# A hybrid decoder step on one core: index scores and top-k of the attention layer moved into its projection blocks

## What is computed

```python
q, k, v, qi, ki, wi = jnp.split(rms_norm(x, g) @ w_in, splits, axis=-1)
q, k = rms_norm(q per head, q_norm), rms_norm(k per head, k_norm)
ki, wi = rms_norm(ki, kidx_norm), wi * (N_IDX_HEADS ** -0.5)
# indexer: 8 heads of 64; the prompt in tiles of 128 queries
dots = einsum('bqhd,bld->bqhl', qi, ki) * (IDX_DIM ** -0.5)
s = where(k_pos <= q_pos, einsum('bqh,bqhl->bql', wi, relu(dots)), -inf)
_, idx = lax.top_k(s, topk)      # prompt: 128 of up to 528; sample: 256 of 2049
o = softmax(q . k[idx]) . v[idx]  # 16 query heads, 4 key heads of 64
x = x + o @ w_attn_out
```

## Time and profile before

| what | us |
|---|---|
| three runs | 2703.45, 2711.70, 2712.51 (median 2711.70) |
| the profiled execution, its own time | 2706.93 |
| its span, first to last instruction | 2705.0 |
| PE busy | 2500.7 (92%) |
| DVE busy | 1299.5 (48%) |
| ACT busy | 733.2 (27%) |
| POOL busy | 780.4 (29%) |
| granted TensorE clock, mean of the span | 0.932 |
| DMA | 250.51 MB, mean 93 GB/s |

### The profile page before, as it was taken

One profiled execution on the slowest core, in us unless ns is written; L12 is line 12 of the kernel. 1 busy time (PEld: TensorE's weight loads), 2 busy tenths in 40 slices (PEclk: granted clock), 3 DMA queues, 4 the chain that ended last, 5 costly groups with the idle time before them and its releaser, 6 DMA issues.

```text
span 2705.0 us, 48495 instructions
## 1 busy us (share of the span) xinstructions
PE 2500.7 (92%) x19842; PEld 2357.9 (87%) x19842; DVE 1299.5 (48%) x1810; ACT 733.2 (27%) x1061; POOL 780.4 (29%) x467
## 2 busy tenths in 40 slices
PE   8999999994399999999999999999979729999999
PEld 8999999861166899999999999999978519999999
DVE  5333354337855353333543333677568753433333
ACT  4122132111033232222322222323656322222222
POOL 3311340024200433123533033400653353331130
PEclk9999999956579999999999999999989759999999
DMA  4323232124422122222322322323440002222222
GB/s 151 101 93 109 78 110 94 47 81 131 134 94 94 63 79 85 86 95 75 111 80 80 105 85 73 133 92 124 149 188 31 32 0 93 94 88 82 94 81 91
DMA packets 60998, 250.51 MB, mean 93 GB/s; under 512 B 9376, under 2 KB 25888, under 8 KB 41056
## 3 DMA queue, kind: packets, MB, share of 16 engines
q1 hardware_dynamic: 56672, 223.94, 23.9%
q0 software_dynamic: 4224, 25.17, 2.8%
HBM read 233.58 MB, written 15.49 MB: 92 GB/s over the span
## 4 chain that ended last, share of the span: by engine, by line
PE 85%; POOL 6%; DVE 4%; issue 3%; ACT 2%; DMA 0%; DVEq 0%; POOLq 0%; ACTq 0%
PE acc L592 49%; PE acc L622 22%; POOL kic L723 2%; PE acc L1689 1%; PE acc L773 1%; PE acc L925 1%; POOL xT L2109 1%; PE acc L934 1%; PE acc L815 1%; PE acc L945 1%; PE acc L1736 1%; PE acc L789 1%; PE acc L914 1%; PE acc L1729 1%; POOL wl L2100 1%
## 5 line engine op out<-in xcount | busy, mean ns | idle before, releaser
L592 PE MATMUL acc<-xh,wh 128*128 128x268 f32 (+1 forms) x3616 | 741.1, 286 | 20.3 <-DVE xl L404 16.4
L592 PE MATMUL acc<-xl,wh 128*128 128x268 f32 (+1 forms) x3616 | 740.8, 286 | 0.0
L592 PE MATMUL acc<-xh,wl 128*128 128x268 f32 (+1 forms) x3616 | 738.5, 285 | 0.0
L592 PEld LDWEIGHTS acc<-xh,wh 128*128 128x128 f32 x3616 | 562.9, 189 | 21.8 <-issue 16.3
L592 PEld LDWEIGHTS acc<-xh,wl 128*128 128x128 f32 x3616 | 563.9, 189 | 0.0
L592 PEld LDWEIGHTS acc<-xl,wh 128*128 128x128 f32 x3616 | 563.1, 189 | 0.0
L395 DVE TENSOR_TENSOR wl<-raw,wh 128x2048 fp32r<-128x2048 f32 x185 | 431.2, 2331 | 203.4 <-ACT wh L336 203.4
L336 ACT ACTIVATE wh<-raw 128x2048 fp32r<-128x2048 f32 x194 | 370.5, 1910 | 544.2 <-PE acc L622 411.0
L547 POOL TENSOR_TENSOR gh<-scr,ones 128x536 f32 (+1 forms) x88 | 94.5, 1074 | 950.1 <-DVE scr L424 950.1
L417 DVE TENSOR_TENSOR scr<-acc,rstd 128x536 f32<-128x536 f32 (+1 forms) x88 | 62.7, 713 | 513.9 <-PE acc L592 513.8
L622 PE MATMUL acc<-gh,wh 128*128 128x268 f32 (+1 forms) x1408 | 288.2, 286 | 0.9 <-POOL gl L548 0.9
(11 more groups left out here) (380 smaller groups left out, 2730.5 us busy)
## 6 DMA issues: line engine op xcount, KB each, us to landing
raw<-in_w_ffn_in SPq DMA_DIRECT2D x88, 1024.0 KB, 4.8
raw<-in_w_ffn_out SPq DMA_DIRECT2D x32, 768.0 KB, 4.2
raw<-in_w_ssd_in SPq DMA_DIRECT2D x21, 1024.0 KB, 4.8
raw<-in_w_ffn_out SPq DMA_DIRECT2D x32, 640.0 KB, 3.9
raw<-in_w_attn_in SPq DMA_DIRECT2D x9, 1024.0 KB, 4.8
kic<-in_kpages SPq DMA_DIRECT2D x64, 128.0 KB, 3.0
xT<-in_state_ssm SPq DMA_DIRECT2D x8, 1024.0 KB, 8.2
out_hs<-xT SPq DMA_DIRECT2D x8, 1024.0 KB, 6.0
```

The source lines that it names most:

```text
L592: mm = nc.tensor.matmul(acc[:, slot * 4 + 2 * t + h, 0:(N - lo) // 2], w[:, slot, c:c + P], x[:, kt, half_of(lo, h)], start=(kt == 0 and w ...
```

## The change

The index queries (chunks 6 and 7) and the index key with the head weights (chunk 8) are made first, then the query, key and value chunks (`IN_ORDER`). From the fourth block on PE goes tile by tile, each tile with two PSUM banks of its own (4, 5 or 6, 7) in place of two blocks of four, so banks 0 to 3 are free for index work, written between the 8 steps of a tile. The index key's norm no longer goes with the other heads: it has its own square, sum, root and inverse within block 3, and the sum over 10 tiles is left. Dots of query tiles 1 and 2 stand in the tiles of block 4, cached dots in blocks 5 and 6, dots of tile 3 in block 7, those of tile 4 behind the blocks. The 16 top-k rounds of tiles 1 and 2 and seven of tile 3 stand between DVE's work for the blocks, the other nine of tile 3 behind them. The 32 counting steps are left with the 16 rounds of tile 4, one in each of the first 16 steps. The transposes of values come behind the dots of tile 4, with waits of PE for the copies between them. Loops of the blocks and of SP's sample keys are written out. Semaphores of the second mixer are renamed or joined, without a change in its order.

```diff
+    IN_ORDER = [6, 7, 8, 0, 1, 2, 3, 4, 5]
+        def tile(p, t, beside=None):
+            n = ATT_IN + p
+            if t == 0:
+                pe.wait_ge(wl_ready, n + 1)
+                pe.wait_ge(tile_read, p - 3) if p > 3 else pe.wait_ge(epilogue_done, ATT_IN + 2 + CREDIT)
+            elif p > 3:
+                pe.wait_ge(epilogue_done, n + CREDIT)
+            for kt in range(DT):
+                mm = products(n, kt, t, 4 + 2 * t)
...
+                if beside:
+                    beside(kt)
+        def dots(j, i):
...
+            if v == 16:
+                pe.wait_ge(own_read, 1)
...
+        block(0, 2)
+        pe.wait_ge(std_ready, norm + 1)
+        block(1, 2)
+        block(2, 1)
+        tile(3, 0, index_keys)
+        turn_weights()
+        tile(3, 1)
+        pe.wait_ge(hw_copied, 2)
...
+        tile(4, 0, lambda kt: dots(1, kt))
+        tile(4, 1, lambda kt: dots(2, kt))
+        tile(5, 0, lambda kt: cached_dots(0, kt))
+        tile(5, 1, lambda kt: cached_dots(2, kt))
+        tile(6, 0, lambda kt: cached_dots(4, kt))
+        tile(6, 1, lambda kt: cached_dots(6, kt))
+        own_dots()
+        tile(7, 0, lambda kt: dots(3, kt))
+        tile(7, 1)
+        tile(8, 0)
+        tile(8, 1)
+        pe.wait_ge(sdots_read, 1)
+        for i in range(NIH):
+            dots(4, i)
...
+        pe.wait_ge(v_copied, 1)
...
+        pe.wait_ge(relu_done, 4 * NIH)
         for n, t in enumerate(NORMED):
...
+        rest(6)
+        rounds(1, 0, 11)
+        out(5, 0)
+        rounds(1, 11, 16)
+        rounds(2, 0, 6)
+        out(5, 1)
+        rest(7)
+        rounds(2, 6, 13)
+        out(6, 0)
+        rounds(2, 13, 16)
+        out(6, 1)
+        rest(8)
+        own_product()
+        weighted(3)
+        out(7, 0)
+        cached_products()
+        sample_keys()
+        out(7, 1)
+        rest(9)
+        rounds(3, 0, 3)
+        out(8, 0)
+        rounds(3, 3, 7)
+        out(8, 1)
+        weighted(4)
...
+        rounds(3, 7, 16)
+        dve.wait_ge(headsq, len(NORMED) + 1)
...
-        for j, q0, w in QTILES:
+        for n in range(32):
+            if n < TOPK_P // 8:
...
+                found = largest(4)
```

More of the change, by code:

```diff
@@ L1195, in dve_attention, with rest, out @@
-        for j, q0, w in QTILES:
+        def rest(p):
+            dve_rest(dve, ATT_IN, 0, p)
+        def out(p, t):
+            n = ATT_IN + p
+            if p > 2 and t == 0:
+                dve.wait_ge(tile_done, p - 2)
+            else:
+                dve.wait_ge(chunk_done, n + 1 + CREDIT)
+            bank = (4 if p > 2 else n % 2 * 4) + 2 * t
+            last = t == 1 or p == 2
+            nc.vector.tensor_tensor(halves(hT[:, 2 * IN_ORDER[p] + t]), acc[:, bank:bank + 2, 0:H], halves(rstd[:]), ALU.mult
+                                    ).then_inc(epilogue_done if last else tile_read if p > 2 else dve_side, 1)
@@ new lines, in rounds, with picked, index_keys @@
+        def rounds(j, first, last):
+            for r in range(first, last):
+                chain.after(take_away(j, largest(j)))
+        def picked(j):
+            _, q0, w = QTILES[j - 1]
+            row = bias[:, j - 1, 0:w]
+            chain.link(nc.vector.tensor_scalar(row, score_row(j), GONE / 1.5, -BIG, ALU.is_gt, ALU.mult))
+            if j == 1:
+                nc.vector.tensor_tensor(row[:, q0:w], row[:, q0:w], negm[:], ALU.add).then_inc(dve_side, 1)
+        def index_keys():
+            dve.wait_ge(ki_sq, 2)
+            chain.link(nc.vector.reciprocal(scr[:, 1], scr[:, 1]))
+            nc.vector.scalar_tensor_tensor(halves(kid[:]), acc[:, 0:2, 0:H], headg[:, 2:3], halves(scr[:, 1]), ALU.mult, ALU.mult
+                                           ).then_inc(ki_ready, 1)
@@ L1237, in dve_attention @@
+        for j in range(1, 4):
+            picked(j)
         dve.wait_ge(sdots_read, 1)
@@ L2281, in _ @@
             if what == "attn":
[L2282 to L2286 removed]
                 act.wait_ge(consts_loaded, 64)
+                act_attention_in(act)
                 act_attention(act)
```

575 lines of the change are left out of this document (313 added, 262 removed).

## The result

The changed kernel takes 2740.34 us (median of four runs, 2738.54 to 2742.49), the kernel before 2708.84 us beside it. The ratio is 1.0106, with a 95% interval from 1.0094 to 1.0118: slower by about 1%, or 31.5 us, where 2675 us and a gain were forecast. The profiled execution took 2738.54 us, with a span of 2736.7.

What follows compares the result with a forecast made beforehand. PE was taken to bound the blocks, key gathers the raw scores, DVE the last counts. Raw scores 21.5 us earlier plus 13.5 saved at the end gave 2706.9 - 35 = 2672, stated as 2675; eight-in-ten range 2656 to 2704.

Steps and rivals of the forecast that it cites:

- rival (a): Blocks: clock falls to half from block 4 to the start of block 7, 72 us become 144; 2744, chance 0.06.
- The term "cached dots": Blocks: cached dots moved onto PE's path, 28.4 us at half clock, so 14.2 if the clock stays full.
- The dots of tiles 1 to 3: Blocks: these dots add 12 us to PE's path at full clock, between bounds of 8.7 and 12.0.
- The wait for `rank`: Blocks, tile 3's first dot in block 7: new PE wait for DVE's own product, 3.5 us, at most 5.
- VectorE costs nothing in the blocks: Blocks: DVE's 68 us from the fourth block on delay nothing, each output being 3 to 4 us early.
- Behind the blocks: From the end of the blocks at 545 us to the first raw scores at 608: 63 us forecast.
- the vnew wait: Behind the blocks, at the value turns: PE newly waits for DVE's copy, 2.3 us.
- Raw scores: First to last raw scores: bound by the samples' key gathers, 69.4 us, unchanged.
- rival (c): Counting stage: key loads are no bound and it shortens with the top-k; 2638, chance 0.06.
- Last raw scores to last count: End of counting: eight counts without top-k rounds, 1.3 us a step, 13.5 us saved.
- Rival (b): Behind the blocks: clock already falls there, head sums take 18.4 us; 2680, inside the forecast's 0.74.
- (e): Whole change: it does not do what it says; only a new unseen wait is left, 2700.

Runs made afterwards that it cites:

- e5_wide: Changed kernel with each cached dot given 64 columns instead of 8, same number and places; 0.9982 of the kernel before.
- e1_no_cached: Changed kernel without the 128 cached dots, eight matmuls of 128 columns standing in; 0.9895 of the kernel before.
- e4_neither: Changed kernel without the 128 cached dots and without the 39 top-k rounds in the blocks; 0.9848 of the kernel before.
- e13_repeat_late: Changed kernel with cached dots' query columns repeated eightfold and first key loads only behind the dots of tile 4; 1.0003 of the kernel before.
- e9_late_keys: e8_early with the first key loads let go only behind the dots of tile 4; 2693.8 us, 0.9941 of the kernel before.
- e10_repeat: Changed kernel with each cached dot's eight query columns repeated up to eightfold by a stride of zero, right result kept; 1.0049 of the kernel before.
- b0_before: The kernel before, run again unchanged for its trace; 0.9995 of the kernel before.
- e8_early: Changed kernel reordered: cached dots in one piece behind tile (4,1), rounds of tiles 1 and 2 beside it, tile 3's dots beside (6,0); 0.9947 of the kernel before.
- after: The changed kernel itself, as first measured; 2740.34 us, 1.0106 of the kernel before.
- e11_best: e9_late_keys with query columns repeated eightfold and raw scores behind every fourth count, not every third; 2685.0 us, 0.9901 of the kernel before.
- e15_best: e11_best again unchanged, in a slow group; 2716.9 us, 0.9880 of the kernel before.
- e3_thin: Changed kernel with cached dots spread 2 or 3 a step over six tiles, key loads only in tile (8,1); 1.0172 of the kernel before.
- e12: Changed kernel with the first key loads let go only behind the dots of tile 4; 1.0080 of the kernel before.
- e14: e11_best with the ten value transposes behind the head sums and their copies behind the reciprocal; 0.9868 of the kernel before.
- e16: e14 again unchanged, in one group with e15_best; 2711.5 us, 0.9858 of the kernel before.

## Why the prediction was wrong

The second part of the working, from the first raw scores on, held. The first failed at the step "so 14.2 if the clock stays full": the clock did not stay full with cached dots between the dense products (0.51 from 482 to 590 us), which cost 33 us, and the dots themselves were sized too small, which cost 31 more.

- *The clock in the blocks.* The forecast laid the cached dots into full-clock blocks and gave rival (a) in full, **2744**, a chance of 0.06. What it describes came about: half clock from 482 to 588 us. That its time was met, 2740, is luck in good part: it charged 72 us to the clock, where 33 are measured below, and had nothing for the terms that make up the rest. Nor would a full clock have saved the forecast: e5_wide keeps it over all four tiles with dots, ends its blocks at 590.2 where 545 was forecast, and is at 0.9982 of the kernel before. The evidence against it was mis-weighed: the second mixer's blocks have no matmuls of 8 columns between their dense ones and the softmax pairs only 16 records of them from 811 to 879 us, while the earlier trace rows already had the very dots in question at 0.51 without an idle gap. Waits did the same elsewhere: behind one of 3.6 us in e1_no_cached, of 2.8 in e4_neither and of 2.4 in e5_wide and e13_repeat_late the clock fell, as behind the 2.37 for `vnew` in the changed kernel, where it was back within 4 us. By the rule on idle gaps that the prediction cites from the Trainium skill (page "TensorE: Matmul & The Clock Gate", section "Why this matters for your kernels") only falls behind a gap had been due; at 529 us before and at 482 us after it fell with no gap. The cost, at the steps' prices: 28 steps with cached dots at 2.61 instead of 1.92 us, and part of one more, are 20, tile (7,0) at 3.26 instead of 1.80 a step (that of e9_late_keys) 12, two steps of (7,1) 1: 33 us.
- *The term "cached dots", 28.4 halved to 14.2.* Mis-sized: they do not get faster with the clock, and each switch to and from dense products costs. 32 steps at 1.17 us are 37, 23 more than the term.
- *The dots of tiles 1 to 3*, 12 us: at full clock a step grew by 0.64, 0.85 and (e9_late_keys) 1.06 us, together 20, so 8 more. Even the bound called upper, which I had taken as the value, was too low; I had no row with dense products beside them.
- *The wait for `rank`*: 3.5 forecast, 1.7 came, though it was 2.8 in e4_neither, at full clock, as the walk had assumed. Sum of these four: 33 + 23 + 8 - 2 = 62, against 59.7 us by which the blocks ended later.
- *VectorE costs nothing in the blocks*: right as it ran, and at full clock too, as long as the dots stand in the tiles (e5_wide, e10_repeat: no wait for `hT`). e1_no_cached, with tiles of 6 us, has 5.0 us of such waits. The forecast's own tiles, 6 us and a quarter of 14.2, lie between, and no run shows them.
- *Behind the blocks* 61.8 us for 63; the vnew wait 2.37 for 2.3; the spreads 1.78 us apart at half clock, as said. *Raw scores* 71.2 for 69.4 with gathers 1.25 us apart: the samples' keys are the bound, rival (c) is out. *Last raw scores to last count* 12.8 for 12.6, so 13.3 of the 13.5 us were saved, by counts 1.3 us apart.
- *Rival (b)* did not happen: the clock fell behind the wait for `vnew` but was back at 622 us, and the head sums took 10.29 us. *(e)*: each piece stood where it was said to be.
- The rest: behind the last count the changed kernel's span has 6.2 us more than that of the earlier trace rows. A second execution of the kernel before (b0_before) has 5.4 more as well, counted from the first pair's score, so this need not be an effect of the change.

## What to carry to other kernels

Before moving small matmuls between dense ones, look how they ran before: ones that run at half clock without a gap may take their new neighbours down with them, and ones whose duration does not follow the clock must not be halved in the sum. Put them in one piece, with the other engines' work beside it, or give them more columns where these are free, and then look again for the waits that the low clock had hidden. When a transfer can start earlier than it is due, look at what runs beside it.

## What the hardware showed beyond that

- A matmul of 64 rows and 8 columns on 32-bit data takes 0.109 us a record in one piece (e8_early), at either clock (e9_late_keys: 31 records in 3 us at 1.00 and at 0.50), and between dense products eight records of 8 columns take 1.04 us, of 64 columns 1.08: up to there width was nearly free.
- With the same count, places and durations, 64 columns held the full clock over 60 us (e5_wide) and 8 columns lost it within 6 (after, 477 to 482.5 us).
- Steps with dots of 144, 272 and 400 columns between dense products held full clock when entered at full (after: 1.00 from 410 to 477 us with the first two, e9_late_keys: 1.00 from 508 to 568 with the third). A tile entered at half with dots in it did not get it back in 26 us (tile (7,0) of after); plain dense ones did in 3 us (after, e9_late_keys, e11_best) to 6 us (e15_best, piece ended at 504.6, clock back at 510.6).
- Beside GpSimd's gathers of keys, TensorE (6.4 us in nine gaps in e8_early, 9.5 in one in e3_thin) and ScalarE (10 to 16 us in e12, e14, e15 and e16) stood still with no engine to wait for. It showed in slow groups only, where the raw scores took 88 to 92 us instead of 72 to 74. The cause is open.
